# A two-block transformer kernel: the first block's early projections in three rounded passes, with the convolution's taps spread otherwise and two loads issued later

## The reference, cut to what matters

```python
h = rmsnorm(x, norm1_g)
z = h @ w_in + b_in                       # 1024 -> 6400 columns
val, gate, q, k, v, g_conv, g_attn = split(z)
# 1. convolution branch
u = val * sigmoid(gate)                   # 256 x 1024
y = depthwise causal conv of u, 31 taps for each channel, + conv_b
y = silu(layernorm(y)) @ w_conv_out
# 2. attention branch: 16 query heads, 2 key/value heads, causal window of 128, a sink for each head
q, k = rope(q), rope(k)
attn = windowed_attention(q, k, v) @ w_attn_o
# 3. merged
x = x + (sigmoid(g_conv) * y + sigmoid(g_attn) * attn) @ w_out
x = x + peer(rmsnorm(x))                  # 16 of 16384 experts for each of 8 heads and token
x = rmsnorm(x)
```

## Time and profile before

| | us |
|---|---|
| median of three runs | 1623.15 |
| profiled execution, its own time | 1624.08 |
| its span | 1622.2 |
| PE busy | 1448.3 (89%) |
| DVE busy | 989.6 (61%) |
| ACT busy | 621.2 (38%) |
| POOL busy | 317.8 (20%) |
| mean granted clock of PE | 0.98 |

### The profile page before, as it was taken

The page is one execution under the profiler, slowest core; times in us unless marked ns, Lnnn a source line. Parts: engine busy times, 40 slices in busy tenths (PEclk is TensorE's granted clock), DMA queues, the critical chain, the costliest instruction groups (busy, mean ns, idle before and its releaser), DMA issues.

```text
span 1622.2 us, 16485 instructions
## 1 busy us (share of the span) xinstructions
PE 1448.3 (89%) x5922; PEld 992.2 (61%) x5922; DVE 989.6 (61%) x1967; ACT 621.2 (38%) x1293; POOL 317.8 (20%) x298
## 2 busy tenths in 40 slices
PE   7999999989987777787988769989999999999998
PEld 5868897644542222333333227867888879778886
DVE  3996776667766767776676453236555455565553
ACT  1014572233333333533333224454444335644442
POOL 2000000334534444434435410400000000000000
PEclk9999999999999999999999989999999999999999
DMA  8345653999999999999999964422545443255451
GB/s 318 130 156 149 126 187 119 422 419 415 414 421 420 420 420 420 415 389 417 410 413 419 420 260 157 152 97 104 207 161 202 147 190 142 86 202 187 176 197 62
DMA packets 51777, 428.55 MB, mean 264 GB/s; under 512 B 6648, under 2 KB 6792, under 8 KB 9584
## 3 DMA queue, kind: packets, MB, share of 16 engines
q0 software_dynamic: 40464, 279.18, 43.1%
q1 hardware_dynamic: 11232, 148.33, 24.1%
HBM read 422.49 MB, written 4.98 MB: 264 GB/s over the span
## 4 chain that ended last, share of the span: by engine, by line
PE 65%; DMA 20%; DVE 8%; ACT 4%; issue 2%; POOL 1%; SPq 0%; DVEq 0%; ACTq 0%; POOLq 0%
DMA pool<-uv,experts 19%; PE psum L741 17%; PE psum L1112 11%; PE psum L871 11%; PE psum L872 10%; PE psum L873 10%; PE psum L774 3%; DVE pool L2037 2%; PE psum L818 2%; DMA ring<-stream 1%; DVE ring_lo L1692 1%; ACT diag L1528 1%; ACT xn L1204 1%; POOL pool L699 1%; ACT coef L1522 1%
## 5 line engine op out<-in xcount | busy, mean ns | idle before, releaser
L1112 PE MATMUL psum<-pool,diag 128*128 128x512 f32 x1024 | 477.0, 615 | 119.9 <-ACT diag L1528 119.8
L2037 DVE CUSTOM_DVE_ANT_0 pool<-pool,xn 128x1024 f32<-128x1024 f32 x256 | 313.3, 1225 | 201.0 <-DMA pool<-uv,experts 199.0
L1112 PEld LDWEIGHTS psum<-pool,diag 128*128 128x128 f32 x1024 | 191.8, 194 | 396.2 <-issue 205.6
L699 POOL DMA_INDIRECT pool<-uv,experts x256 | 286.5, 1119 | 505.3 <-PE psum L1112 357.6
L1692 DVE TENSOR_TENSOR ring_lo<-ring,w_hi 128x2048 fp32r<-128x2048 f32 x76 | 173.9, 2292 | 114.0 <-ACT w_hi L1296 114.0
L741 PE MATMUL psum<-hT,ring 128*128 128x256 f32 (+1 forms) x832 | 175.0, 371 | 5.9 <-DMA ring<-stream 4.1
L1518 ACT ACTIVATE acts<-dots 128x2 f32<-128x2 f32 x128 | 26.0, 203 | 379.5 <-DVE dots L2037 379.4
L1296 ACT ACTIVATE w_hi<-ring 128x2048 fp32r<-128x2048 f32 x76 | 144.4, 1908 | 65.5 <-PE psum L873 37.7
L741 PEld LDWEIGHTS psum<-hT,ring 128*128 128x128 f32 x832 | 151.7, 196 | 28.6 <-issue 8.2
L871 PE MATMUL psum<-w_hi,h_hi 128*128 128x512 f32 x400 | 161.3, 403 | 5.1 <-DVE h_lo L1731 4.2
L872 PE MATMUL psum<-ring_lo,h_hi 128*128 128x512 f32 x400 | 157.5, 394 | 0.0
(11 more groups left out here) (267 smaller groups left out, 1858.4 us busy)
## 6 DMA issues: line engine op xcount, KB each, us to landing
ring<-stream SPq DMA_DIRECT2D x66, 2048.0 KB, 7.7
pool<-uv,experts POOLq DMA_INDIRECT x256, 12.7
ring<-stream SPq DMA_DIRECT2D x3, 1024.0 KB, 4.8
t_scratch<-tab POOLq DMA_DIRECT2D x1, 2048.0 KB, 56.8
rpb_scratch<-tab POOLq DMA_DIRECT2D x1, 1792.0 KB, 22.9
ring<-stream SPq DMA_DIRECT2D x1, 1792.0 KB, 6.9
row<-rows POOLq DMA_DIRECT2D x1, 1672.0 KB, 15.5
ring<-stream SPq DMA_DIRECT2D x1, 1664.0 KB, 6.5
```

Source lines behind the costliest of these rows:

```text
L699: gp.indirect_dma_start(out=gath[:, n % NROWS, :], out_offset=None, in_=uv, in_offset=bass.IndirectOffsetOnAxis(ap=experts[:, n:n + 1], ax ...
L1112: last = nc.tensor.matmul(psum[:, RB + half, :], diag[:, n % NDIAG, :], gath[:, n % NROWS, D + 512 * half:D + 512 * half + 512], start=k = ...
L2037: ins = V.tensor_tensor_reduce(out=row_u, in0=row_u, in1=xn[:, n // SLOTS, :], scale=1.0, scalar=0.0, op0=ALU.mult, op1=ALU.add, accum_out ...
```

## The change

- The chunks of `glu` are laid out anew: a bank now holds the value and the gate of one block of 128 channels, where before one bank held two values and the next two gates. The sigmoid (ACT) and the product (DVE) are done for one block at a time, and the taps of a block can begin after its bank.
- glu chunks 1 to 3, both chunks of q and the chunk of k and v go through `split_products`. Eleven parts are split: 6 of glu, 4 of q, 1 of k and v. The normed input is split as well (`n_hi` by ACT, `n_lo` by DVE). Chunk 0 of glu stays in float32. The gate blocks stay in float32.
- The taps: 3, 7, 7, 7, 7, 7, 7, 4 after the eight blocks, 22 ahead of the last split and 24 behind it, 34 after the rotation, 8 in each head.
- `row` and `keys` are issued after the `rpb` loads have landed and glu's second bank is filled.
- Twelve idle products (128x128 by 128x256, float32, overwritten) stand ahead of PE's wait for the second tile of `mix0`, and six ahead of PE's wait in the second layer's first pair.

```diff
-TAPS_AFTER_GLU = (28, 31, 31, 80)
-TAPS_AFTER_ROPE = 12
-TAPS_IN_HEAD = 5
+TAPS_AFTER_GLU = (3, 7, 7, 7, 7, 7, 7, 4)
+TAPS_BEFORE_KV, TAPS_AFTER_KV = 22, 24
+TAPS_AFTER_ROPE = 34
+TAPS_IN_HEAD = 8
+WARM_MIX_NORM, WARM_PAIR = 12, 6
+EARLY = (("glu", 1), ("glu", 2), ("glu", 3), ("q1", 0), ("q1", 1), ("kv1", 0))
+EARLY_GLU, EARLY_Q, EARLY_KV, EARLY_PARTS = 0, 6, 10, 11
+NEARLY = 4
...
@@ gpsimd
-            gp.dma_start(row[:, :], rows.to_broadcast([P, NROW])).then_inc(row_landed, 16)
-            gp.dma_start(keys.rearrange("p m n -> p (m n)"), keys_in).then_inc(keys_landed, 16)
...
             gp.wait_ge(rpb_landed, 16 * HEADS2)
+            gp.wait_ge(bank_filled, FILL_NO["glu", 0, 1] + 1)
+            gp.dma_start(row[:, :], rows.to_broadcast([P, NROW])).then_inc(row_landed, 16)
+            gp.dma_start(keys.rearrange("p m n -> p (m n)"), keys_in).then_inc(keys_landed, 16)
@@ tensor
+            def begin_warm(name, count):
+                dst = begin(name)
+                for _ in range(count):
+                    nc.tensor.matmul(dst[:, 0:S], ident, cst[:, 0:S], start=True, stop=True)
+                return dst
...
-            feature_major("glu", 4)
-            token_major_chunks("q1", 2, hT)
-            token_major_chunks("kv1", 1, hT, 256)
+            feature_major("glu", 1)
+            pe.wait_ge(normed_split, 1)
+            normed_halves = (n_hi, n_lo)
+            for q in range(EARLY_GLU, EARLY_Q):
+                split_feature_major(-2, q, normed_halves)
+            for i in range(2):
+                for t in range(NT):
+                    tile_products(("q1", i), -2, EARLY_Q + 2 * i, normed_halves, t)
+            w_kv = wait_part(-2, EARLY_KV)
+            for t in range(NT):
+                kv = begin(("kv1", 0, t))
+                for k in range(KD):
+                    last = split_products(kv[:, 0:256], [v[:, k, tile128(t)] for v in normed_halves],
+                                          [v[:, k, :] for v in w_kv], k == 0, k == KD - 1)
+                last.then_inc(bank_filled, 1)
...
-            tile_transposes("mix0", 1, xn[:, 1, :])
+            tile_transposes("mix0", 1, xn[:, 1, :], WARM_MIX_NORM)
@@ scalar
+            for t in range(NT):
+                for hf in range(2):
+                    wait_emptied(act, ("N1", t, hf))
+            nc.scalar.activation(n_hi[:, :, :], hT[:, :, :], ACT.Copy).then_inc(normed_high, 1)
...
+            nc.scalar.activation(unused, eps, ACT.Sigmoid)
+            act.wait_ge(bank_filled, FILL_NO[("t5",)] + 1)
+            split_high(-2, 0)
+            for m in range(KD):
+                b = wait_filled(act, ("glu", m // 2, m % 2))
+                nc.scalar.activation(glu_sig[:, m, :], b[:, S:2 * S], ACT.Sigmoid, bias=par_("b_glu")[:, KD + m:KD + m + 1]
+                                     ).then_inc(sigmoid_ready, 1)
+                split_high(-2, m + 1)
+            split_high(-2, KD + 1)
             for i in range(2):
                 for t in range(NT):
                     empty(("q1", i, t), qkv[:, t, 512 * i:512 * i + 512])
+                if i == 0:
+                    split_high(-2, EARLY_KV)
@@ vector
+            dve.wait_ge(normed_high, 1)
+            V.tensor_tensor(n_lo[:, :, :], hT[:, :, :], n_hi[:, :, :].bitcast(F32), ALU.subtract).then_inc(normed_split, 1)
+            split_low(-2, 0)
...
+            for m in range(KD):
+                dve.wait_ge(sigmoid_ready, m + 1)
+                name = ("glu", m // 2, m % 2)
+                b = wait_filled(dve, name)
+                V.scalar_tensor_tensor(u[:, m, TAPS - 1:], b[:, 0:S], par_("b_glu")[:, m:m + 1], glu_sig[:, m, :],
+                                       ALU.add, ALU.mult).then_inc(emptied_sem(name), 1)
+                wait_emptied(dve, name)
+                block_ready[0] = m + 1
+                split_low(-2, m + 1)
+                conv_taps(TAPS_AFTER_GLU[m])
+            split_low(-2, KD + 1)
+            conv_taps(TAPS_BEFORE_KV)
+            split_low(-2, EARLY_KV)
+            conv_taps(TAPS_AFTER_KV)
```

More of the change, by code:

```diff
@@ L230, in part_chunk @@
 def part_chunk(layer, q):
+    if layer == -2:
+        return EARLY[q // 2], q % 2
     if layer < 0:
@@ L268, in part_slot @@
 def part_slot(layer, q):
+    if layer == -2:
+        return q % NEARLY
     if layer < 0:
@@ L768, in token_major_chunks, with transposes @@
                     token_major(name, i, w, act, KD, n)
-            def transposes(name, sources, rows_out=P):
-                dst = begin(name)
+            def transposes(name, sources, rows_out=P, dst=None):
+                if dst is None:
+                    dst = begin(name)
                 for j, src in enumerate(sources):
@@ L775, in transposes, with tile_transposes @@
                 last.then_inc(bank_filled, 1)
-            def tile_transposes(name, t, src):
+            def tile_transposes(name, t, src, warm=0):
+                first = begin_warm((name, t, 0), warm) if warm else None
                 pe.wait_ge(xn_ready, xn_before[name] + t + 1)
                 for hf in range(2):
-                    transposes((name, t, hf), [src[:, P * k:P * k + P] for k in range(4 * hf, 4 * hf + 4)])
+                    transposes((name, t, hf), [src[:, P * k:P * k + P] for k in range(4 * hf, 4 * hf + 4)],
+                               dst=None if hf else first)
             def wait_tile(name, t):
@@ L907, in first_pair @@
             def first_pair(first, second, layer, q, halves, norm, split_before):
+                dst = begin_warm(first + (0,), WARM_PAIR) if layer == 1 and q == 0 else begin(first + (0,))
                 pe.wait_ge(h_split, split_before + 2)
-                tile_products(first, layer, q, halves, 0)
+                tile_products(first, layer, q, halves, 0, dst)
                 tile_transposes(norm, 1, normed_rows(1))
@@ new lines, in _ @@
+            V.tensor_tensor(n_lo[:, :, :], hT[:, :, :], n_hi[:, :, :].bitcast(F32), ALU.subtract).then_inc(normed_split, 1)
+            split_low(-2, 0)
+            taps_done, tap_step, block_ready = [0] * KD, [0] * KD, [0]
+            turn_taken = [0]
+            def conv_taps(count):
+                for _ in range(count):
+                    open_blocks = [m for m in range(block_ready[0]) if taps_done[m] < TAPS][:2]
+                    if not open_blocks:
+                        return
+                    turn_taken[0] += 1
+                    m = open_blocks[turn_taken[0] % len(open_blocks)]
+                    w = taps_done[m]
+                    taps_done[m] += 1
+                    src, tap = u[:, m, w:w + S], conv_w[:, m, w:w + 1]
+                    if w:
+                        after(tap_step[m])
+                        ins = V.scalar_tensor_tensor(y[:, m, :], src, tap, y[:, m, :], ALU.mult, ALU.add)
+                    else:
+                        ins = V.tensor_scalar(y[:, m, :], src, tap, par_("conv_b")[:, m:m + 1], ALU.mult, ALU.add)
+                    if w == TAPS - 1:
+                        ins.then_inc(conv_ready, 1)
+                    else:
+                        tap_step[m] = mark(ins)
@@ L2234 @@
     for i in range(4):
-        parts["glu", i] = by_k(np.concatenate([w_in[:, 256 * i:256 * i + 256], w_in[:, 1024 + 256 * i:1280 + 256 * i]], 1))
+        parts["glu", i] = by_k(np.concatenate([w_in[:, D * side + P * m:D * side + P * m + P]
+                                               for m in (2 * i, 2 * i + 1) for side in range(2)], 1))
         parts["gate", i] = by_k(w_in[:, 3328 + 512 * i:3840 + 512 * i])
```

57 lines of the change are left out of this document (18 added, 39 removed).

## The result

The changed kernel takes 1614.35 us (median of 6 runs, 1612.4 to 1617.24), beside 1625.06 for the kernel before (6 runs). The ratio is 0.9935, with a 95% interval from 0.992 to 0.9949: 10.6 us faster, between 8.3 and 13. Its profiled execution took 1612.64 us, with a span of 1610.8, 11.4 less than the span before.

A forecast was written before the change was run, and what follows sets the result against it. PE bounds the kernel almost to the attention's end, then DVE's added work would set that point: 1624.08 - 9.3 - 2.6 = 1612.2, less 0.9 for the profiled execution lying over the median, gives 1611.3 us, range 1607 to 1615.

The forecast's parts named there:

- the mark: DVE's mean at the end of the attention, 193.50 us before; whatever moves it moves the rest of the program.
- DVE sets the mark, by its sum: From glu's second bank to the last division: 150.3 us of DVE work plus 4.2 of waits, ending at 184.2, 9.3 sooner.
- rival A: PE sets the mark and all 19 us come through: 1601.4 us; chance 4%.
- PE's start: PE's first glu product at 12.5 instead of 17.20, 4.7 us sooner, with `row` and `keys` loaded later.
- the slow first stretch: Chunk 0's 64 instructions on PE: 16.8 us against 13.9 at full pace, 2.9 us of slowness kept.
- The passes: Three passes in glu, q, k and v: 14.5 us off PE; k and v done at 90.8, 19 us sooner.
- Chunk 3: Glu's chunk 3, issued together with `row` and `keys`, lands late: 0.9 us of DVE waits, bounds 0 and 3.
- The idle products: Twelve before the norm of mix0's second tile: gain 2.6 us if the clock stays, 0 if it falls.
- The six in the second layer: Six idle products in a 2.8 us wait with the clock at 1.00: no gain, bounds -0.2 and +0.3.
- PE's idle spell before `attno`: After the heads: 3.05 us before, longer by 1; a slow spell there costs 0 to 1.7 us, taken as 0.
- Rival C: PE's waits for DVE in the heads lower its clock, lengthening the heads; 1655 us if wholly at 1.2 GHz; chance 4%.
- Rivals B and D: B: half the gain lost to late supply, mark moves 4.6, 1616 us, 12%. D: nothing measurable, within 0.2%, 2%.

The follow-up runs named there:

- late_loads_only: Kernel before, with only `row` and `keys` issued after the rpb loads and glu's second bank: 1618.96 us, ratio 0.9961.
- the gaps filled: Changed kernel with 14 idle products instead of 12 before the norm of mix0's second tile, 2 more between its transposes and first chunk: 1611.86 us, 0.992.

## Why the prediction was right, and where it was off

The time before, 1623.15, was the median of three runs; with three more it is 1625.06. Against that the change was 10.7 us; the prediction had 11.8. The mechanism was the forecast one. That the terms agree to some tenths is partly luck: the mark itself scatters by 1 us between profiles, and several errors below cancel.

- *DVE sets the mark, by its sum.* Shown. Predicted 184.2, found 184.53; work predicted 150.3, DVE's busy time from 29 to 184 is 149.9. Taking DVE work out in all heads moved the mark by 9.6 us, and PE's unbroken chain, on which rival A stood, said nothing about what comes next when PE is made faster.
- *PE's start.* Predicted 12.5, found 13.28. I had overlooked PE's product for the bias table, 1.87 us, which the wait for the chunk had covered, and the chunk itself lands at 13.3 and not at 12.0. In exchange the slow first stretch cost 15.74 - 13.9 = 1.8 us and not 2.9. The two errors cancel: second bank predicted at 29.3, DVE's new work at 29.7, found 29.56.
- *The passes.* k and v were done at 90.8 by the prediction, and the gate blocks behind them began at 90.8 in PE's timeline; the first scores came at 117.99, predicted 118.
- *Chunk 3.* I gave it 0.9 us of DVE's waits (and 29.3 + 10 + 2 is 41.3, not the 41.8 that I wrote). ACT began the fourth block's rounding at 40.79 with no wait at all:

```profile
40.42 0.48 ACT L1458 ACTIVATE pool<-psum,par 128x256 f32<-128x256 f32 x1 [3.38 <-PE psum L904]
40.79 1.91 ACT L1341 ACTIVATE e_hi<-ring 128x2048 fp32r<-128x2048 f32 x1
```

  From 29.56 on DVE was idle for 5.0 us all the same, instead of 4.2 (the 1.4 us for the sigmoid in the list above lie ahead of 29.56): 1.4 for the rounding in the second block (predicted 1.5), 0.2 for each of six further roundings instead of 0.1, 0.8 at the first scores, 0.4 at the first division, 0.6 at the mean, and the rest in small pieces between instructions.
- *The idle products.* 2.6 predicted, 1.0 found in the profile of the changed kernel. The prediction said that they "leave 1 us of idling" and that the gain is 2.6 us "if the clock stays, 0 if it falls all the same". The transposes did gain their 0.9; behind them the clock fell, and the 1.7 us of the chunk instructions came to 0.3. It had also overlooked a second gap, 1.0 us between the transposes and the chunk. In five of eight profiles with these products the clock stayed at 1.00, and the stretch was 28.7 us instead of 31.4: there the whole 2.6 came. So the size was right where its condition held, and for the condition the prediction gave no odds. The six in the second layer: the granted clock of that stretch was 1.00 in all ten profiles that have them. Of the three without them, it fell in that of `late_loads_only` (0.63 in the 4 us from 1312), and PE reached the next transposes 7.2 us after the wait instead of 5.7. No run took the six out alone; what they do by themselves stays untested.
- *PE's idle spell before `attno`.* The prediction called it the largest unknown and had it longer by 1 us. It was 2.95 us instead of 3.05. Before, the granted clock was 0.57 in the 4 us from 200, behind that wait; in the changed kernel it was 1.00 in the windows behind it, and the lead grew from 9.0 to 9.7 us. Nothing in the prediction foresaw that.
- *The 1.6 us near 1405.* No step of mine had them. The windows at the end of the third attention, before and after:

```profile
1405.00:1409.00 4.00, 3.74 (x10) 3.01 (x11) 4.00 (x3) 3.98 (x3) 0.00 (x0) 0.57 0.00 0
```

```profile
1396.00:1400.00 4.00, 4.00 (x18) 3.27 (x18) 4.00 (x3) 3.98 (x3) 0.00 (x0) 1.00 0.00 0
```

  Before, the clock fell there and PE got 10 instructions done where it now did 18. With the gaps filled, in a kernel that is the changed one but for those few instructions, it fell again:

```profile
1393.00:1397.00 4.00, 3.90 (x10) 3.11 (x11) 4.00 (x2) 3.98 (x3) 0.00 (x0) 0.57 0.00 0
```

  Of the twelve other profiles, all but that of `late_loads_only` have the dip. So I take it for luck of the one profiled execution, which also was 1.7 us under the median of its kernel. That is argued from the profiles, not tested.
- *Rival C* was there in part. The clock fell twice in the heads, behind waits of PE for ACT of 1.53 and 1.39 us. The windows of both:

```profile
150.00:154.00 4.00, 4.00 (x14) 3.38 (x14) 4.00 (x14) 0.90 (x4) 0.00 (x0) 0.60 0.53 55
180.00:184.00 4.00, 4.00 (x22) 4.00 (x22) 3.84 (x5) 2.89 (x3) 0.00 (x0) 0.57 0.47 49
```

  DVE stayed full through the first, and what it cost is DVE's 0.4 us of wait at the first division. The second lies just ahead of the mark: PE's 12 products and 8 transposes there took 2.35 and 1.91 us, where with the gaps filled they took 1.59 and 1.04, and DVE waited 0.62 us for them at the mark, which it didn't there. So a slow PE cost about 1 us in all, and nothing where it was the one that waited. The rule of the Trainium skill that I had set against the trace ("TensorE: Matmul & The Clock Gate", "A second HAM failure mode: psum-queue depth-cycling") speaks of small idle spells from going round the PSUM banks. The trace agrees that short idle spells in the heads go with a falling clock, but the two waits ahead of the falls were for ACT, and they didn't set the time. Rivals B and D did not happen.

## What to carry to other kernels

Before making the fullest engine cheaper, add up the busy time of the one that gets the extra work, over the whole stretch up to the point where both meet: its free time is all that can be gained, and half of PE's 19 us ended as waiting. Then set the size of the change by the balance: eight parts in three passes, with the taps spread to fit, were better than eleven, since by the sums the last three cost DVE 2.2 us each to save PE 1.3. Filler work has to be spread so that each stage is balanced and not only the sum; the same taps in another place went with a mark 4 us later. And before a fall of the clock in one profile is put down to a gap, look whether the other profiles with the same gap have it.

## What the hardware showed that I had not expected

- The same two gaps of 1.1 and 1.0 us around eight transposes, behind 5.3 us of products without a pause, went with a fall of the granted clock in three profiles (0.57 in the 4 us from 962 in the changed kernel, 1.7 us lost) and with 1.00 throughout in five. In the experts, gaps of 1.3 us between bursts of full-width products left it at 1.00. What decides between them no run here shows.
- A POOL that does elementwise work slows DVE's taps from 480 to 702 ns, and takes over 2 us for the same tap.
- The instruction pace shows a slow first stretch for which the granted column says 1.00; with PE busy without a pause from the transposes on, it is over before 17 us.
